# Four chains in lockstep instead of two and two, and 32x32 blocks, in the chunk stages of a gated recurrence (one core of Trainium2)

## What is computed

```
def step(S, inp):
    w_t, k_t, v_t, a_t, b_t = inp[:5]
    sa = jnp.einsum('bhij,bhj->bhi', S, a_t)
    S = S * w_t[:, :, None, :] + sa[..., None] * b_t[:, :, None, :] + v_t[..., None] * k_t[:, :, None, :]
    y = jnp.einsum('bhij,bhj->bhi', S, inp[5]) if emit else None
    return S, y
S, ys = lax.scan(step, state0, xs, reverse=reverse)
```

## Time and profile before

| | us |
|---|---|
| three executions, median (lowest to highest) | 2367.19 (2364.46 to 2368.46) |
| the profiled execution, its own time | 2364.71 |
| its span (first to last instruction) | 2362.9 |
| PE, DVE, ACT, POOL busy in the span | 1795.5, 842.9, 644.1, 268.7 |
| granted TensorE clock, mean | 0.88 of 2.4 GHz |

### The profile page before, as it was taken

One profiled execution on the slowest core, in us unless ns is written; L12 is line 12 of the kernel. 1 busy time (PEld: TensorE's weight loads), 2 busy tenths in 40 slices (PEclk: granted clock), 3 DMA queues, 4 the chain that ended last, 5 costly groups with the idle time before them and its releaser, 6 DMA issues. The chain is left out here.

```text
span 2362.9 us, 35691 instructions
## 1 busy us (share of the span) xinstructions
PE 1795.5 (76%) x15437; PEld 1227.8 (52%) x15437; DVE 842.9 (36%) x1231; ACT 644.1 (27%) x1035; POOL 268.7 (11%) x330
## 2 busy tenths in 40 slices
PE   6998988978999877798888977555566565655555
PEld 6997987867778766697777862111111111111111
DVE  4654445765555466577564642000000000000001
ACT  4334445554333344333432430000000000000001
POOL 0100014420211043201450000000000000000000
PEclk9999998999999888898996988888777877888887
DMA  6654642337996410051002449999999999999996
GB/s 202 197 181 145 194 153 72 96 133 235 298 294 210 150 42 2 19 184 59 3 3 75 163 160 408 429 427 428 428 428 428 428 428 427 429 427 428 428 427 295
DMA packets 178551, 588.56 MB, mean 249 GB/s; under 512 B 8131, under 2 KB 141326, under 8 KB 153822
## 3 DMA queue, kind: packets, MB, share of 16 engines
q1 hardware_dynamic: 177026, 585.38, 64.3%
q10 hardware_dynamic: 1372, 0.92, 0.2%
HBM read 584.99 MB, written 1.28 MB: 248 GB/s over the span
## 5 line engine op out<-in xcount | busy, mean ns | idle before, releaser
L3351 PE MATMUL ps<-ex_ring,ex_xe 128*32 128x512 f32 x1440 | 223.8, 754 | 167.9 <-DMA ex_ring<-in_exp_w 167.9
L3424 DVE TENSOR_TENSOR ex_hid<-ps,ex_silu 128x512 f32<-128x512 f32 x16 | 11.1, 692 | 867.3 <-PE ps L3351 867.3
L3351 PEld LDWEIGHTS ps<-ex_ring,ex_xe 128*32 128x32 f32 x1440 | 44.1, 124 | 340.2 <-DMA ex_ring<-in_exp_w 253.2
L209 PE MATMUL ps<-xt_hi,ffn_whi 128*128 128x256 f32 x704 | 205.0, 291 | 7.3 <-DVE xt_lo L372 7.3
L210 PE MATMUL ps<-xt_lo,ffn_whi 128*128 128x256 f32 x704 | 200.6, 285 | 0.0
L211 PE MATMUL ps<-xt_hi,ffn_wlo 128*128 128x256 f32 x704 | 200.3, 285 | 0.0
L181 DVE TENSOR_TENSOR ffn_wlo<-ring,ffn_whi 128x2048 fp32r<-128x2048 f32 x66 | 154.3, 2338 | 113.8 <-ACT ffn_whi L174 113.4
L3373 PE MATMUL ps<-ex_ring,ex_ht 128*32 128x512 f32 x688 | 119.0, 826 | 68.5 <-DMA ex_ring<-in_exp_w 61.1
L174 ACT CAST ffn_whi<-ring 128x2048 fp32r<-128x2048 f32 x66 | 125.2, 1901 | 110.9 <-PE ps L211 95.4
L209 PEld LDWEIGHTS ps<-xt_hi,ffn_whi 128*128 128x128 f32 x704 | 137.3, 195 | 17.2 <-issue 16.6
L210 PEld LDWEIGHTS ps<-xt_lo,ffn_whi 128*128 128x128 f32 x704 | 136.9, 195 | 1.5 <-issue 1.5
(11 more groups left out here) (772 smaller groups left out, 4145.0 us busy)
## 6 DMA issues: line engine op xcount, KB each, us to landing
ex_ring<-in_exp_w SPq DMA_DIRECT2D x133, 2048.0 KB, 46.0
ring<-in_exp_w SPq DMA_DIRECT2D x40, 2048.0 KB, 45.6
ring<-in_w_in SPq DMA_DIRECT2D x55, 1024.0 KB, 5.3
ex_late<-in_exp_w SPq DMA_DIRECT2D x19, 2048.0 KB, 46.9
ring<-in_ffn_w_gate SPq DMA_DIRECT2D x22, 1024.0 KB, 6.1
ring<-in_ffn_w_up SPq DMA_DIRECT2D x22, 1024.0 KB, 5.4
ring<-in_ffn_w_down SPq DMA_DIRECT2D x22, 1024.0 KB, 5.0
ffn_mod_tile<-in_mod_w SPq DMA_DIRECT2D x12, 1024.0 KB, 7.4
```

What stands on the lines that cost most here:

```text
L209: nc.tensor.matmul(out, lhs[0], rhs[0], start=start, stop=False, skip_group_check=shared)
L3351: mm = mm_(ps[32 * q:32 * q + 32, 4 + u, :], xe[:, k], w[:, 512 * q:512 * q + 512], start=k == 0, stop=k == KC - 1)
L3424: v.tensor_tensor(hid[:], ps[:, 5, :], silu[:], ALU.mult).then_inc(S["hid"], 1)
```

## The change

It rewrites `recurrence_chunks` and turns one loop in `States.pe_step`.

1. `order()` runs all four chains round by round. Each chain has two PSUM banks, used in turn, and its own copy of every SBUF tile (`NQ` = 4); several tiles share storage (`both`, `front`, `pair`).
2. Round 0's loops are turned: the same kind of product for all 4 chunks and both halves of the rows, then the next kind. Before, all products of a chunk were issued one behind the other.
3. `off` is no longer made by DVE but by ACT (L2726 of the new file, 16 of 32 columns). `yt3` goes from DVE to ACT, and round 4's result is copied whole by ACT as 32x32 blocks (one instruction in place of three).
4. In rounds 5 to 8 the four 32x32 diagonal blocks are multiplied one by one (`by_chunks`): 16 matmuls of 32 rows and 32 columns per round and chain in place of 4 of 128x128. POOL no longer lays out `off_s` and `p3_s`, and makes `g2` with one instruction for a chain instead of four.
5. The last round becomes rounds 9 to 12: `rm` for chunks 0 and 2, then 1 and 3, ACT's copy, then `tm` and `g1` for 0 and 2, then 1 and 3, and DVE's adds.
6. In `pe_step` the two halves of the rows alternate in the state's matmuls; before, 4 of one half came first.

```diff
 
-CHUNK_ROUNDS = 10
...
+        its = [(t, h4) for t in range(TT) for h4 in range(2)]
+        NQ = len(its)
+
+        raw = sb("raw", [P, NQ, 4, 5 * CH])
+        off = sb("off", [P, NQ, 4, CH])
+        both = sb("both", [P, NQ, 8 * P])
+        front = sb("front", [P, NQ, 12 * CH])
+        pair = sb("pair", [P, NQ, 2, 4, CH])
...
+        RAW, SPREAD, FLIPPED, TWO, LOW3, FTIL, KM = 1, 2, 4, 6, 7, 8, 9
+        G2 = KM if ctx_only else KM + 1
+
+        KEPT, HIGH, YT3, FACTOR, F1, COUPLED, RM = 2, 3, 6, 7, 8, 9, 10
...
         def order():
-            for it in range(0, len(its), 2):
-                for r in range(CHUNK_ROUNDS):
-                    for j in range(2):
-                        yield its[it + j], r, it + j
+            for r in range(CHUNK_ROUNDS):
+                for q in range(len(its)):
+                    yield q, r
...
-        def bank(h4, r):
-            return 4 * h4 + 3 - r % 2
...
+        def bank(q, r):
+            return ps[:, 2 * q + (r + 1) % 2, :]
...
+        def by_chunk(q):
+            return ps[:, 2 * q:2 * q + 2, :].rearrange("p b (c n) -> p (b c) n", c=2)
...
+            def by_chunks(out, hs, left, right):
+
+                for c in range(4):
+                    mm = mm_(out[group(c), wide * hs:wide * hs + wide], left[group(c)], right[group(c)], start=True, stop=True)
+                return mm
+
+            for q, r in order():
+                (t, h4), out = its[q], bank(q, r)
+                by_dve, by_act = S[f"by_dve{q}"], S[f"by_act{q}"]
                 if r == 0:
-                    if n >= 2:
-                        pe.wait_ge(S[f"rm_copied{h4}"], n // 2)
+                    for k in range(2):
+                        for kind in range(2 if ctx_only else 3):
+                            for c in range(4):
+                                for e in range(2):
+                                    half, pr = slice(HD * e, HD * e + HD), 2 * h4 + k
+                                    tok_c = slice(P * t + CH * c, P * t + CH * c + CH)
+                                    a, bb = ar[half, pr, :, tok_c], bk[half, pr, :, tok_c]
+                                    out = ps[group(c), 2 * q + e, 256 * k:256 * k + n_raw]
+                                    if kind == 0:
+                                        mm = mm_(out[:, 0:64], a[:, 0], bb[:, 0:2], start=True, stop=True)
+                                    elif ctx_only:
+                                        mm = mm_(out[:, 64:96], bb[:, 0], a[:, 0], start=True, stop=True)
+                                    elif kind == 1:
+                                        mm = mm_(out[:, 64:128], bb[:, 0], a[:, 0:2], start=True, stop=True)
+                                    else:
+                                        mm = mm_(out[:, 128:160], bb[:, 1], a[:, 1], start=True, stop=True)
...
-                        for hs in (0, 2, 1, 3):
-                            e, k = hs // 2, hs % 2
-                            half, pr = slice(HD * e, HD * e + HD), 2 * h4 + k
-                            tok_c = slice(P * t + CH * c, P * t + CH * c + CH)
-                            a, bb = ar[half, pr, :, tok_c], bk[half, pr, :, tok_c]
-                            out = ps[group(c), 4 * h4 + e, 256 * k:256 * k + n_raw]
-                            mm_(out[:, 0:64], a[:, 0], bb[:, 0:2], start=True, stop=True)
-                            if ctx_only:
-                                mm = mm_(out[:, 64:96], bb[:, 0], a[:, 0], start=True, stop=True)
-                            else:
-                                mm_(out[:, 64:128], bb[:, 0], a[:, 0:2], start=True, stop=True)
-                                mm = mm_(out[:, 128:160], bb[:, 1], a[:, 1], start=True, stop=True)
...
                 elif r == 5:
+                    pe.wait_ge(by_act, FACTOR)
                     if not ctx_only:
-                        pe.wait_ge(S[f"joined{h4}"], n // 2 + 1)
+                        pe.wait_ge(S["joined"], q + 1)
                     for hs in range(4):
-                        right = tok[:, 1, t, head_columns(h4, hs)] if ctx_only else f1[:, s, hs]
-                        mm = mm_(out[:, wide * hs:wide * hs + wide], spread[:, s, 0, hs], right, start=True, stop=True)
+                        right = tok[:, 1, t, head_columns(h4, hs)] if ctx_only else f1(q)[:, hs]
+                        mm = by_chunks(out, hs, factor(q)[:, hs], right)
                 elif r == 6:
-                    pe.wait_ge(S[f"f1_copied{h4}"], n // 2 + 1)
-                    pe.wait_ge(S[f"expanded{h4}"], 3 * (n // 2) + 2)
+                    pe.wait_ge(by_act, F1)
                     for hs in range(4):
-                        mm = mm_(out[:, wide * hs:wide * hs + wide], off_s[:, s, hs], f1[:, s, hs], start=True, stop=True)
+                        mm = by_chunks(out, hs, off[:, q, hs], f1(q)[:, hs])
                 elif r == 7:
-                    pe.wait_ge(S[f"coupled{h4}"], n // 2 + 1)
+                    pe.wait_ge(by_act, COUPLED)
                     for hs in range(4):
-                        mm = mm_(out[:, wide * hs:wide * hs + wide], spread[:, s, 0, hs], coupled[:, s, hs], start=True, stop=True)
+                        mm = by_chunks(out, hs, factor(q)[:, hs], coupled(q)[:, hs])
                 elif r == 8:
-                    pe.wait_ge(S[f"expanded{h4}"], 3 * (n // 2) + 3)
+                    pe.wait_ge(by_dve, FTIL)
                     for hs in range(4):
-                        mm = mm_(out[:, wide * hs:wide * hs + wide], p3_s[:, s, hs], ftil[:, s, hs], start=True, stop=True)
+                        mm = by_chunks(out, hs, raw[:, q, hs, CH:2 * CH], ftil(q)[:, hs])
...
-                    for hs in range(4):
-                        for c in range(4):
-                            e, k = hs // 2, hs % 2
-                            rows, half, cols = group(c), slice(HD * e, HD * e + HD), head_columns(h4, hs)
-                            out = ps[half, 4 * h4 + c, :]
-                            mm_(out[:, 96 * k:96 * k + wide], tok[rows, 0, t, cols], ftil[rows, s, hs], start=True, stop=True)
-                            mm = mm_(out[:, 192 + HD * k:192 + HD * k + HD], km[rows, s, hs], vtok[rows, t, cols],
-                                     start=True, stop=True)
...
+                    if r == 9:
+                        pe.wait_ge(by_dve, G2)
+                    elif r == 11:
+                        pe.wait_ge(by_act, RM)
+                    else:
+                        pe.wait_ge(S[f"pe{q}"], r)
+                    for k in range(2):
+                        for c in ((0, 2), (1, 3))[(r + 1) % 2]:
+                            for e in range(2):
+                                hs, rows, out = 2 * e + k, group(c), by_chunk(q)[HD * e:HD * e + HD, c]
+                                cols = head_columns(h4, hs)
+                                if r < 11:
+                                    mm = mm_(out[:, HD * k:HD * k + HD], coupled(q)[rows, hs, 0:HD], vtok[rows, t, cols], start=True, stop=True)
+                                else:
+                                    mm = mm_(out[:, 96 * k:96 * k + wide], tok[rows, 0, t, cols], ftil(q)[rows, hs], start=True, stop=True)
+                mm.then_inc(S[f"pe{q}"], 1)
...
+            nc.scalar.activation(pair[:, :, 1], eye.unsqueeze(1).unsqueeze(1).to_broadcast([P, NQ, 4, CH]), ACT.Copy, scale=-1.0
+                                 ).then_inc(S["minus"], 1)
+            over, edge = (slice(16, CH), CH - 1) if d else (slice(0, 16), 0)
+            for q, r in order():
+                (t, h4), done = its[q], S[f"by_act{q}"]
...
+                act.wait_ge(S[f"pe{q}"], r + 1)
                 if r == 0:
...
+                        ins = nc.scalar.copy(spread(q)[group(c), 1, :, group(c)], raw[group(c), q, :, 2 * CH:3 * CH])
+                    ins.then_inc(done, 1)
+                    act.wait_ge(S[f"by_dve{q}"], SPREAD)
+                    ins = nc.scalar.activation(off[:, q, :, over], own(q)[:, :, over], ACT.Copy,
+                                               scale=g.masks[:, d, 160 + edge:161 + edge])
...
+                    if r == 3:
+                        ins.then_inc(done, 1)
+                        act.wait_ge(S[f"by_dve{q}"], LOW3)
+                        ins = nc.scalar.copy(yt3(q).rearrange("p c j -> p (c j)"), bank(q, r)[:, 0:P])
+                elif r == 4:
+                    ins = nc.scalar.copy(both[:, q, 0:P], bank(q, r)[:, 0:P])
+                elif r == 5:
+                    ins = nc.scalar.copy(front[:, q, 0:4 * wide], bank(q, r)[:, 0:4 * wide])
                 elif r == 6:
...
+                    ins = nc.scalar.copy(both[:, q, P:P + 4 * wide], bank(q, r)[:, 0:4 * wide])
...
+                    ins = nc.scalar.copy(rm[:, 4 * t:4 * t + 4, 2 * h4:2 * h4 + 2],
+                                         by_chunk(q)[:, :, 0:P].rearrange("p c (k e) -> p c k e", k=2))
...
+                if r in (4, 5, 6, 9, 10, 11):
...
```

(19 more changed lines are left out.)

258 lines of the change are left out of this document (112 added, 146 removed).

## The result

The changed kernel took 2350.99 us in the median of 5 executions (2350.14 to 2356.41), the kernel before 2367.19 in the same comparison (2362.64 to 2368.46): ratio 0.993, 95% interval 0.9915 to 0.9945. That is 16.2 us less, where 38 were forecast. Two later comparisons of the same kernel gave 0.9908 (0.9888 to 0.9929) and 0.9919 (0.9905 to 0.9934).

What follows compares the result with a forecast made beforehand. The end was taken to follow the weight stream's start, held up by the chunk stages. Savings 6.8 + 7.1 + 8.0 + 8.9 + 7.4 = 38.2 us, from 2364.7 to 2326.5, as a median 2329; range 2311 to 2356.

Steps and rivals of the forecast that it cites:

- The end is the stream's start, one for one: Start of the experts' weight loads: each microsecond a chunk stage saves moves it, and the kernel's end, one for one.
- Rounds 0 to 4: First rounds of a chunk stage, filled by ACT and DVE: round 5 starts at 21.2 us (context) or 23.0 (latent).
- Rounds 5 to 8: 32x32 block products on PE: 7.2 us a context stage, before 14.6; 10.2 a latent stage, before 15.7.
- the prediction's own sign of being wrong: The prediction called itself wrong if a record costs 25 ns or more; it took 14 to 20 ns in rounds 5 to 8.
- Rounds 9 to 12: Last parts and DVE's adds: 27 ns a record, 12 parts in 5.2 us; then 0.7 plus 2.8 (context) or 4.4 (latent).
- State moves: Turned loop in the state's matmuls: saves 0.32 us a move, 23 of 28 moves on the path, 7.4 us.
- The lengths before: Chunk stages of the old kernel, taken from windows with a margin: 43.9, 44.2, 51.5 and 52.4 us.
- the small blocks gain nothing: Rival for rounds 5 to 8: 16 small pairs cost as much as 4 large; 25.8 us back, 2355, chance 0.14.
- Groups of rows wait for one bank: Rival for rounds 5 to 8: only one group of rows can write a bank; +102 us, 2431, chance 0.04.
- The clock falls: Rival for rounds 5 to 12: a quarter-filled array drops the clock to 0.50; +56 us, 2385, chance 0.05.

Runs made afterwards that it cites:

- the run with large products: The changed kernel with rounds 5 to 8 as four 128x128 products, their left operand from a tile needing no laying out: 2344.18 us, ratio 0.9898.
- the chunk stages alone: The changed kernel with the old loop of the state moves put back: 2360.62 us, ratio 0.9972 to the kernel before.
- the run that filled them: The changed kernel with one more 128x128 product, read by nobody, in each chain-round of rounds 5 to 8: 2366.06 us, ratio 0.9997.

## Why the prediction was right and wrong

1. *The end is the stream's start, one for one:* right (14.3 us earlier at the start, 13.6 shorter in all).
2. *Rounds 0 to 4* (21.2 and 23.0 us): 19.6 to 20.6 and 23.2 to 24.1, right within 1.6 us. (Round 3's sum, printed as 2.5, is 2.75; the 20.8 behind it has it right.) The order of DVE's and ACT's work gave the number, although PE waited for instructions in round 0, since it was ahead of them.
3. *Rounds 5 to 8* (7.2 and 10.2): **this is the step that failed**, as "so I take 14 ns for 64 columns and 20 for 96 ... 16 x 0.45 = 7.2 us". The record was priced rightly: 14.0 ns from start to start between stalls in rc, 0.66 us a chain-round in rl (forecast 0.64). What was missing is the supply. Four rounds of four chains are 256 products, 512 records of MATMUL and as many of LDWEIGHTS: 1024 instructions, four blocks of 256. At 3.5 to 4.0 us a block that is 14 to 16 us, less what is in store at the start; measured 15.4, 15.2, 13.1 and 13.5. Excess over the forecast 8.2 + 8.0 + 2.9 + 3.3 = 22.4 us. The rows that I took the 14 ns from the earlier trace rows were a burst of 64 records, half a block. The pace of a burst that has been fetched beforehand is none for a stream of 512. Over the whole of rounds 5 to 8 a record took 15.4 us / 512 = 30 ns, and the prediction's own sign of being wrong (25 ns or more) came true.
4. *Rounds 9 to 12* (8.7 and 10.3): 8.6, 8.7, 10.0, 11.1. The number is right by luck. The forecast has 27 ns for a record; at the full clock and with instructions at hand it is some 14 to 16, and these rounds take 6.7 to 8.3 (the run with large products). Waits for instructions and the half clock made up the rest.
5. *State moves* (7.4): 7.5 by the stretches of the kernel with nothing else changed, and 6.9 between the chunk stages alone and the change. Right, and the only term that I had from a direct comparison of two rows, though 23 moves on the path was a count and not read from a row.
6. *The stretches behind the stages:* I had no term for them. The chunk stages alone made them 5.5 us longer, in a trace with a lower clock there; that the clock is the cause is argued and not shown.
7. *The lengths before* were taken 0.5 to 0.6 us too long, 2.3 in all, and the shorter way from the last add to what comes next (0.4 us for 1.2, so 3.2 in all) was not counted. The two nearly cancel, which is luck too.

Sum: 38.2 - 22.4 - 5.5 = 10.3 of forecast by these steps; the trace has 11.2 in the stretches that the change touches (9.8 in the stages, 1.4 behind them), 3.1 less ahead of rc0, where nothing was changed (rc0 starts at 866.1, 870.1 and 866.8 in three profiled executions of the change, at 869.1 in the one of before), and 0.7 more behind the stream's start. The measured 2351 lies inside the range, 2311 to 2356, but near the place of the rival that comes next and not of the forecast.

Of the rivals, *the small blocks gain nothing* named the queue as one possible cause and priced it at 25.8 us back, for 2355; what was lost was 22.4. I gave it 0.14 because of the 14 ns. *Groups of rows wait for one bank* is refuted: four groups write one bank at 14.0 ns a record from start to start. What the Trainium skill says in "TensorEngine Tiling (Array Packing)", Gotcha 1, on row tiles and one PSUM bank does not hold here as a pace. *The clock falls* was half right: it fell, but in the last rounds and behind the stage, and perhaps by PE's standing still, as the run with large products suggests (clock 0.99 and 1.00 in rc). By step 6 it cost some 5 us, and not 56. That the stalls are what lowers it was not shown apart: the run that filled them added too much work.

The Trainium skill bears on step 3 in "Runtime: NRT & Kernel Launch", section Instruction fetch mechanics. It says that instructions come in blocks of 16 KiB, 256 of them, which the trace shows: 16 KB packets, a stall behind each 128 pairs. It also says that the fetch is hidden behind the time that instructions take to issue. The trace disagrees for PE: a block of short matmuls is gone in 2.0 us, and the next one is there after 4.0. Had I held the number of added instructions against the size of a block, I would have asked for the time of a block, which the missing term rests on.

## What to carry to other kernels

Before cutting a large matmul into small ones, count PE's instructions (a matmul in fp32 is four here) and give each 256 of them 3.5 to 4 us, as measured here: that is a floor for the stretch, which a burst shorter than a block doesn't show. Where the floor binds, mix rounds of few large products with rounds of many small ones, so that work and supply come closer; here that made the context stages shorter in the traces, and a gain of the whole over the change was not shown. Time the small edits (here one turned loop in the state moves) on their own: it was worth about half of the whole.

## What was not expected of the hardware

- PE's instructions: 256 in 3.5 to 4.0 us, so 14 to 16 ns for an instruction and about 30 for a pair of LDWEIGHTS and MATMUL, with 64 columns (14.0 ns a record) as with 32; stalls up to 2.6 us, shown only as "issue". The fetch of a block started 1.1 us after PE took up the one before, although its queue was idle.
- A 32x32 tile takes 56 ns for a record of 64 columns at the full clock, as worked out from 27.8 ns a record with two tiles in turn and 14.0 with four: they work side by side without loss, although all of them write one bank.
- The stretch between rl0 and rl1 takes 24 us or 33, with the same instructions, by the granted clock (mean 0.93 or 0.55). It differs between executions of one kernel, so single executions differ by 9 us, and medians of five can move with it.
- Behind rl1 the clock stood at its half level for 37.5 us before and 44.4 us in the change (from round 9 of rl1 on), though PE was busy for most of it, 31.3 and 35.3 us; with denser products among the moves it stayed there through all seven in one run, and came back after four in the other.
